# A hybrid encoder layer on one core: the input projections' stage reordered, and the scatter's row numbers computed beside the expert's output

## What is computed

```python
mod = silu(c) @ ada_w + ada_b                  # six rows of 1024: sh1, sc1, gt1, sh2, sc2, gt2
u = layer_norm(x) * (1 + sc1) + sh1
p_rw, p_conv, p_gate = split(u @ w_in)         # 27 + 16 + 16 tiles of 128 columns
p_rw = p_rw + mu_prev*(prev - p_rw) + mu_next*(next - p_rw)      # neighbours in time
h = h_a * sigmoid(h_b)                         # h_a, h_b: halves of p_conv
h = silu(layer_norm(depthwise_conv31(h)))
y_b = h @ cpw_w + cpw_b
y_a = rwkv7(p_rw)                              # scans in both directions
x1 = layer_norm(alpha*x + (1 + gt1) * ((g_a*y_a + g_b*y_b) @ w_o))
u2 = layer_norm(x1) * (1 + sc2) + sh2
# each token goes to 8 of 64 experts, F = 256, and to one shared expert:
y = sum_k weight_k * (silu(u2 @ gate_e) * (u2 @ up_e)) @ down_e + shared
out = layer_norm(alpha*x1 + (1 + gt2) * y)
```

## Time and profile before

| | us |
|---|---|
| median of three runs | 2157.51 |
| lowest, highest | 2155.03, 2160.31 |
| the profiled execution | 2165.9 |
| its span, first to last instruction | 2164.2 |
| TensorE busy | 1928.5 (89% of the span) |
| VectorE busy | 1399.5 (65%) |
| ScalarE busy | 880.3 (41%) |
| GpSimd busy | 660.9 (31%) |
| mean granted clock of TensorE | 0.956 of 2.4 GHz |

### The profile page before, as it was taken

How to read it: one execution, slowest core, us unless ns; L and a number is a source line. 1 busy time by engine, 2 the same in 40 slices (tenths; PEclk the granted TensorE clock), 3 DMA queues, 4 the chain that set the end, 5 groups by cost and what they waited for, 6 DMA issues and landing times. The chain is left out here.

```text
span 2164.2 us, 54389 instructions
## 1 busy us (share of the span) xinstructions
PE 1928.5 (89%) x20438; PEld 1424.8 (66%) x20438; DVE 1399.5 (65%) x2791; ACT 880.3 (41%) x1464; POOL 660.9 (31%) x533
## 2 busy tenths in 40 slices
PE   5699999978399999999997788999999999999966
PEld 1576777746298998999894355666666666666632
DVE  2688788844254656565642847777777777777717
ACT  0322232222245454555431005555555555555501
POOL 4545444301534344434410301221122222122213
PEclk9899999989599999999998888999999999999988
DMA  5644554214200010001005118899889888888845
GB/s 198 209 132 145 179 167 151 80 53 132 70 21 10 17 32 26 26 14 32 14 14 189 65 51 342 325 344 328 329 323 337 314 318 328 315 326 326 319 168 215
DMA packets 161938, 377.90 MB, mean 175 GB/s; under 512 B 23572, under 2 KB 97474, under 8 KB 134385
## 3 DMA queue, kind: packets, MB, share of 16 engines
q1 hardware_dynamic: 140292, 337.50, 43.6%
q0 software_dynamic: 21152, 37.80, 4.9%
q10 hardware_dynamic: 335, 0.22, 0.0%
HBM read 361.00 MB, written 53.24 MB: 191 GB/s over the span
## 5 line engine op out<-in xcount | busy, mean ns | idle before, releaser
L1991 DVE TENSOR_TENSOR moe_w_lo<-moe_raw,moe_w_hi 128x1024 fp32r<-128x1024 f32 x272 | 315.0, 1221 | 2.5 <-ACT moe_w_hi L1910 2.1
L1910 ACT ACTIVATE moe_w_hi<-moe_raw 128x1024 fp32r<-128x1024 f32 x272 | 265.3, 1047 | 85.8 <-DMA moe_raw<-in_exp_up 83.9
L1854 PE MATMUL moe_pH<-moe_w_hi,moe_x_hi 128*128 128x512 f32 x544 | 221.1, 406 | 38.7 <-DVE moe_x_lo L1998 29.4
L1788 POOL DMA_INDIRECT moe_xg<-scratch_u2d,moe_idx x70 | 70.9, 1012 | 588.5 <-issue 513.4
L1864 PE MATMUL moe_pY<-moe_wd,moe_hT 128*128 128x512 f32 x544 | 244.8, 593 | 0.5 <-ACT moe_hT L1925 0.5
L419 POOL TENSOR_TENSOR proj_w_lo<-proj_w,proj_w_hi 128x1024 fp32r<-128x1024 f32 x59 | 177.2, 3008 | 211.3 <-ACT proj_w_hi L503 211.3
L621 DVE SCALAR_TENSOR_TENSOR proj_hc<-proj_hp,cwT,proj_hc 128x256 f32 x480 | 232.3, 557 | 7.9 <-DVE proj_st L594 7.9
L446 PE MATMUL proj_bank<-proj_u_hi,proj_w_hi 128*128 128x512 f32 x536 | 211.9, 395 | 24.5 <-DVE proj_u_lo L652 12.2
L1854 PE MATMUL moe_pH<-moe_w_hi,moe_x_lo 128*128 128x512 f32 x544 | 213.8, 393 | 0.0
L1854 PE MATMUL moe_pH<-moe_w_lo,moe_x_hi 128*128 128x512 f32 x544 | 213.5, 393 | 0.0
L446 PE MATMUL proj_bank<-proj_u_hi,proj_w_lo 128*128 128x512 f32 x536 | 210.6, 393 | 0.0
(11 more groups left out here) (337 smaller groups left out, 3679.5 us busy)
## 6 DMA issues: line engine op xcount, KB each, us to landing
moe_raw<-in_exp_gate SPq DMA_DIRECT2D x69, 1024.0 KB, 7.0
moe_raw<-in_exp_up SPq DMA_DIRECT2D x69, 1024.0 KB, 10.0
moe_wd<-in_exp_down SPq DMA_DIRECT2D x68, 1024.0 KB
proj_w<-in_w_in SPq DMA_DIRECT2D x59, 512.0 KB, 4.6
proj_aw<-in_ada_w SPq DMA_DIRECT2D x8, 2048.0 KB, 8.2
last_yb<-scratch_ybuf SPq DMA_DIRECT2D x4, 2560.0 KB, 25.0
mod_aw<-in_ada_w SPq DMA_DIRECT2D x4, 2048.0 KB, 19.6
scratch_rkv<-proj_st SPq DMA_DIRECT2D x24, 256.0 KB, 2.2
```

The lines of the kernel that those rows point to most:

```text
L1788: pool.indirect_dma_start(out=xg[q][:], out_offset=None, in_=g["u2d"][:], in_offset=bass.IndirectOffsetOnAxis(ap=idx[q][:, 0:1], axis=0), ...
L1854: ins = nc.tensor.matmul(pH[:], a[:, k], w[p][:, k].rearrange("p w f -> p (w f)"), start=(k == 0 and n == 0), stop=(k == KC - 1 and n == 2))
L1910: nc.scalar.activation(w_hi[p][:, ks].rearrange("p k w f -> p w k f"), raw[p][:, :, ks], ACT.Copy) \
L1991: nc.vector.tensor_tensor(w_lo[p][:, ks].rearrange("p k w f -> p w k f"), raw[p][:, :, ks], w_hi[p][:, ks].rearrange("p k w f -> p w k f") ...
```

## The change

Three stages' code is touched.

In `modulation_and_norm` the modulation is made as columns: ada_w is the stationary operand in pieces of 128x128 and one column of silu(c) the moving one, 4 x 8 matmuls for each of the four loaded groups of 512 columns, in two halves (groups 0 and 2, then 1 and 3). Each half's bias is added from a transposed row, and four of the eight channel tiles of u are turned and scaled after each half; the way over memory is gone. The stage also makes the high and low halves of u, loads the first five tiles of w_in, makes four high and two low halves of them, and xn takes x's place.

In `projections_and_conv` the loop over trips is replaced by one list of 67 tiles in another order (hb and ha alternating, then ga, gb, then r, k, v, then lora, then cpw), with four slots for halves, five for raw weights, six PSUM banks and six slots for stores. VectorE makes all low halves instead of GpSimd. The taps are 512 wide, two channel tiles alternate, and a planner (`tap_plan`) gives each tile's place a quota of them. The convolution's mean is made in four parts between products, centring to silu beside later products. The other modulation rows are made like the first ones: eight pieces of 4 x 8 matmuls with 128x128 stationary and one moving column, after tiles 20, 23, ... 41. gb stays in SBUF in u1T's place.

In `moe` place_y is gone: the destination rows are written in read_y, directly before the output's second half, `gcol` and the semaphore y_ready are gone, and ScalarE and VectorE take the weight from `val`.

```diff
 def modulation_and_norm(...)
+        bcol = s.sb("bcol", [P, 2, KC])
+        u1 = g["u1T"]
...
-            for n in range(NG):
+            for n in (0, 2, 1, 3):
                 sp.dma_start(aw[:, n], ada_w[0, :, n * GROUP:(n + 1) * GROUP]...).then_inc(aw_in[n], 16)
-            sp.dma_start(bias[:], ada_b[:, 0:2 * D]).then_inc(b_in, 16)
-            sp.wait_ge(row_done, NG)
-            sp.dma_start(g["mod"][:, 0:2 * D], row[:]).then_inc(row_out, 16)
-            sp.wait_ge(row_out, 16)
-            for n in range(2):
-                sp.dma_start(mod[:, n], columns(g["mod"][0, n * D:(n + 1) * D])).then_inc(mod_in, 16)
+            for n in range(RAW):
+                sp.dma_start(g["w"][:, n], weight_tile(w_in, None, n)).then_inc(w_pre, 16)
...
+            for k in range(KC):                                          # ScalarE
+                act.wait_ge(tp_used, k + 1)
+                nc.scalar.activation(g["u_hi"][:, k], u1[:, k], ACT.Copy).then_inc(tp_high, 1)
+            act.wait_ge(w_pre, 16 * RAW)
+            for n in range(SPLIT):
+                nc.scalar.activation(g["w_hi"][:, n], g["w"][:, n], ACT.Copy).then_inc(w_high, 1)
...
-            for n in range(NG):                                          # TensorE
-                pe.wait_ge(aw_in[n], 16)
-                for k in range(KC):
-                    ins = nc.tensor.matmul(acc[n][0:1, :], g["csil"][:, k:k + 1], aw[:, n, k], ...)
+            for h in range(2):
+                for n in (h, 2 + h):
+                    pe.wait_ge(aw_in[n], 16)
+                    for m in range(GROUP // P):
+                        col = (n // 2) * 4 + m
+                        for k in range(KC):
+                            ins = nc.tensor.matmul(acc[h][:, col:col + 1], aw[:, n, k, m * P:(m + 1) * P], g["csil"][:, k:k + 1], ...)
                 ins.then_inc(mod_done, 1)
+                if h == 0:
+                    pe.wait_ge(xn_done, TT)
+                for k in range(4 * h, 4 * h + 4):
+                    ...
+                    turn(k)
...
+TILES = [(kind, i) for i in range(KC) for kind in ("hb", "ha")] \
+    + [("ga", i) for i in range(KC)] + [("gb", i) for i in range(KC)] \
+    + [(kind, i) for i in range(KC) for kind in RKV] + [("lora", j) for j in range(3)]
+N_U = len(TILES)
+TILES += [("cpw", n) for n in range(KC)]
+RAW, SPLIT, BANKS_P, N_ST = 5, 4, 6, 6
+MOD_AFTER = list(range(20, 44, 3))
+def tap_plan():
+    work = {"ha": 0.7, "r": 1.7, "k": 1.7, "v": 1.7, "lora": 1.7}
+    quota, ends, credit, done = [], [], 0.0, 0
+    for n in range(N_U):
+        credit += 5.45 + (3.6 if n in MOD_AFTER else 0.0) - 1.3 - (work.get(TILES[n - 1][0], 0.0) if n else 2.5)
+        there = 2 * CW * (n // 4)
+        q = max(0, min(int(credit / 0.67), there - done, KC * CW - done))
...
 def projections_and_conv(...)
-            def modulate(i):
-                for k in range(KC):
-                    ins = nc.tensor.matmul(pstat[0:1, :], g["csil"][:, k:k + 1], aw[:, k], ...)
+            def modulate(c):
+                pe.wait_ge(aw_at[c % 2], 16 * (c // 2 + 1))
+                for m in range(MC):
+                    col = c * MC + m
+                    for k in range(KC):
+                        ins = nc.tensor.matmul(pmod[:, col:col + 1], aw[:, c % 2, k, m * P:(m + 1) * P], g["csil"][:, k:k + 1], ...)
+                ins.then_inc(S["mod_done"], 1)
+            for n in range(N):
+                product(n)
+                for q in range(KC // 2):
+                    if n == ends[q] + 1:
+                        mean(q)
+                if n in MOD_AFTER:
+                    modulate(MOD_AFTER.index(n))
...
+                if n == E_CONV + 3:
+                    variance()
...
+            def high_h():                                                # ScalarE, before the cpw tiles
+                act.wait_ge(S["tile_done"], N_U)
+                for k in range(KC):
+                    act.wait_ge(S["silu"], k + 1)
+                    nc.scalar.activation(u_hi[:, k], hc[:, k], ACT.Copy).then_inc(S["h_high"], 1)
...
+            for n in range(N + 1):                                       # VectorE
+                if n == N_U:
+                    split_h()
+                if n >= 1:
+                    evict(n - 1)
+                if SPLIT <= n + 3 < N:
+                    low(n + 3)
+                if n < N_U:
+                    taps(quota[n])
...
 def moe(...)
             def read_y(b, q, n):                                         # ScalarE
                 act.wait_ge(d_done, 2 * b + 1)
-                act.wait_ge(y_ready, b + 1)
+                act.wait_ge(i_ready, b + 1)
                 act.wait_ge(y_free[q], n + 1)
-                nc.scalar.activation(y[q][:, 0:512], pY[0][:], ACT.Copy, scale=gcol[q][:, 0:1]).then_inc(y0_read, 1)
+                nc.scalar.activation(y[q][:, 0:512], pY[0][:], ACT.Copy, scale=val[:, bass.ds(b, 1), 2]).then_inc(y0_read, 1)
-            def place_y(b, q, n):                                        # VectorE
-                v.wait_ge(y_free[q], n + 1)
-                v.wait_ge(y0_read, b)
-                ch.mark(nc.vector.tensor_scalar(sidx[q][:], val[:, bass.ds(b, 1), 1], float(NO_ROW), None, ALU.add))
-                nc.vector.tensor_copy(gcol[q][:], val[:, bass.ds(b, 1), 2]).then_inc(y_ready, 1)
             def read_y(b, q, n):
                 v.wait_ge(y_free[q], n + 1)
                 v.wait_ge(d_done, 2 * b + 2)
-                v.wait_ge(y_ready, b + 1)
-                nc.vector.tensor_scalar(y[q][:, 512:D], pY[1][:], gcol[q][:, 0:1], None, ALU.mult).then_inc(y1_read, 1)
+                ch.mark(nc.vector.tensor_scalar(sidx[q][:], val[:, bass.ds(b, 1), 1], float(NO_ROW), None, ALU.add))
+                nc.vector.tensor_scalar(y[q][:, 512:D], pY[1][:], val[:, bass.ds(b, 1), 2], None, ALU.mult).then_inc(y1_read, 1)
             def body(b, p, i):
                 ...
                 read_y(b - 1, 1 - p, i + (p - 1))
-                place_y(b, p, i)
```

More of the change, by code:

```diff
@@ new lines, in projections_and_conv @@
+        st = s.sb("st", [P, N_ST, T])
+        gb = g["u1T"]
+        rs = s.sb("rs", [P, T])
+        bank = [s.ps(f"bank{i}") for i in range(BANKS_P)]
+        pstat, pmod = s.ps("pstat"), s.ps("pmod")
+        w_at = [s.sem(f"w_at{i}") for i in range(RAW)]
+        aw_at = [s.sem(f"aw_at{i}") for i in range(2)]
+        stored = [s.sem(f"stored{i}") for i in range(N_ST)]
+        taken = [s.sem(f"taken{i}") for i in range(BANKS_P)]
+        names = """w_high w_low tile_done base_done padded taps conv_done mean_done cent sq_done var_done std_done
+            rs_done nrm silu h_high h_split mod_done modc_done turned mrow_done mod_out brow_in""".split()
@@ new lines, in _ @@
+            sp.dma_start(brow[:], ada_b[0, 2 * D:].rearrange("(r p) -> r p", p=P)).then_inc(S["brow_in"], 16)
+            for n in range(RAW, N + RAW + 3):
+                if n < N:
+                    load(n)
+                if n == RAW + 2:
+                    load_mod(0)
+                if n == RAW + 4:
+                    load_mod(1)
+                m = n - RAW - 3
+                if m in slot_of:
+                    store(m)
+                if m in MOD_AFTER and MOD_AFTER.index(m) + 2 < KC:
+                    load_mod(MOD_AFTER.index(m) + 2)
+                if m == N_U:
+                    sp.wait_ge(S["mrow_done"], 1)
+                    sp.dma_start(g["mod"][0, 2 * D:].rearrange("(r p) -> r p", p=P), mrow[:]).then_inc(S["mod_out"], 16)
@@ L441, in _ @@
+            for slot in range(N_ST):
+                sp.wait_ge(stored[slot], 16 * len([n for n in keeps if slot_of[n][0] == slot]))
+            sp.wait_ge(S["mod_out"], 16)
         @block.tensor
         def _(pe):
-            def product(o, j, k):
-                for n, (a, b) in enumerate(((w_hi, u_hi), (w_lo, u_hi), (w_hi, u_lo))):
-                    ins = nc.tensor.matmul(o[:], a[:, j, k], b[:, k], start=(k == 0 and n == 0),
-                                           stop=(k == KC - 1 and n == 2))
-                return ins
@@ L467, in _ @@
-            for j in range(NK):
-                project(j, 0, None)
-            modulate(0)
-            with pe.Fori(1, KC) as i:
-                for j in range(NK):
-                    project(j, i, i)
-                modulate(i)
-            for j in range(3):
-                project(j, KC, KC)
-            pe.wait_ge(mod_read, KC + 1)
-            pe.wait_ge(h_used, KC + 1)
-            for k in range(KC):
-                ins = nc.tensor.matmul(pstat[:], g["mean1024"][:], hc[:, k], start=(k == 0), stop=(k == KC - 1))
@@ new lines, in high_h @@
+            def high_h():
+                act.wait_ge(S["tile_done"], N_U)
+                for k in range(KC):
+                    act.wait_ge(S["silu"], k + 1)
+                    nc.scalar.activation(u_hi[:, k], hc[:, k], ACT.Copy).then_inc(S["h_high"], 1)
+            for n in range(N):
+                if n == N_U:
```

(18 more changed lines are left out.)

552 lines of the change are left out of this document (236 added, 316 removed).

## The result

The changed kernel takes 2188.2 us (median of five runs, 2176.16 to 2194.12) against 2160.31 us of the kernel before (five runs beside it, 2155.03 to 2163.97): ratio 1.0118, 95% interval 1.0095 to 1.0141. It is slower by 28 us, where 2150 was forecast. The profiled execution is the fastest of the five (2176.16), so a sum over its stages comes out 12 us low.

The account below looks back on a forecast made before the run. TensorE, 89% busy, was taken as the bound. Terms +18.3, +26.7, -1 and -51.6 sum to -7.6: profiled 2165.9 becomes 2158.3, less 8.4 to the median gives 2150 us; range 2080 to 2202, the forecast's own 2118 to 2187.

Parts of the forecast that it names:

- The opening: Opening: the modulation's weight loads run at half clock, first product at 91.8 instead of 73.47: +18.3 us.
- The modulations in the projections: Projections: eight modulations between products lose the full clock, 13.5 us each, 108 in all; stage +26.7 us.
- The convolution's norm under the products: Projections: centring, squares, root and silu run beside products; 1.7 us lost before the first cpw tile.
- Rival (d): Projections: VectorE becomes the bound if a tap costs over 0.8 us; up to 2200 us; chance 0.04 together with others.
- The experts: Experts' stage: without VectorE's wait landings get quicker and the block period falls from 11.2 to 10.45 us: -51.6 us.
- Rival (a): Experts: GpSimd's serial gather, scatter, landing keeps the period at 11.2 us, decisive if above 10.55; 2201 us; chance 0.19.
- (b): Opening and projections: TensorE's clock does not fall, opening -8, projections -20; 2077 us; chance 0.12.
- (c): Opening and projections: clock kept and a modulation costs only the planner's 3.6 us; 2036 us; chance 0.03.

Follow-up runs that it names:

- the front alone: The changed kernel with the old experts' stage, so only opening and projections are changed; median 2202.93 us, ratio 1.0184 to the kernel before.
- the late landing and the added wait: The changed kernel, GpSimd waiting for scatter b-2's landing, its sign ahead of the scatter, gather held until hidden(b+1) is done; 2146.47 us, ratio 0.9922.
- The small doses: The changed kernel with the projections' 256 modulation pairs in 32 pieces of 8, one after each of tiles 20 to 51; 2152.55 us, ratio 0.9938.
- the late landing alone: The changed kernel with GpSimd waiting for the landing of scatter b-2 instead of b-1; median 2171.93 us, ratio 1.0053 to the kernel before.

## Why the prediction was wrong

**The opening** was right, with its reason: half clock, 0.213 us a load, first product at 90.87 for a forecast of 91.8. The terms that the prediction names add to 91.1, not 91.8 (84.6 + 1.4 + 4.2 + 0.9), so 0.7 us of the forecast has no term behind it.

**The modulations in the projections** were right in mechanism and a little dear: 10.5 and 2.2 behind make 12.7 where 13.5 was forecast, 6 us in all. The full clock lasted 3 us into the first, as taken (2.9). The scan came at +34.9 against +44; by medians, with the front alone, the whole kernel lost 40.

**The convolution's norm under the products** was right. No tile waits for a low half, and the one wait ahead of the cpw tiles is 1.5 us. Rival (d) did not come.

**The experts** are the step that failed: "I take 10.45 as the period, nearer the unhindered row: -51.6". The period came out at 10.86 in the changed kernel's profile, its fastest run; by medians the edit gave -22 alone and -15 in the changed kernel. The mechanism I had named is shown in part: in the good stretch landings are quicker (7.4 instead of 8.3) and most blocks take 10.25. That the place among the loads is the reason is not shown there, since the gather starts 2.8 us after the issue of gate and up in the good stretch and 2.4 in the kernel before; only the run with the late landing and the added wait moves the place on purpose. What failed was to take the good stretch as where the chain comes to rest. Nothing holds it there. Gather and scatter (2.6 us) and a landing of 4.3 to 12.0 come to the period or over it, so a few slow landings push GpSimd past the good place, landings there are 9.3, the lag grows until a gather is late, and TensorE loses 3 us and part of its clock (granted 0.72 on average over the 6.2 us behind). With the landing taken out of the series this lag and the wide spread are gone. The wait that I saw removed had been the regulator: with it the mean stayed at 11.2. Rival (a), the serial chain, had the right cause at 0.19, and the period stayed above its mark of 10.55, but its price was too high; the result lies between it (2201) and the forecast. I had both numbers, the sum of 11 us and the spread 4.9 to 11.8, and read the spread as a chance for gain alone.

The forecast's own range fails with it: its bounds for the experts, -65 to -22, leave out the -15, and with those for the front they add to 2120.5 to 2195.5, not to the 2118 to 2187 that it states.

**Rivals (b) and (c)**, clock kept, fell with the first stretch at 0.50. The small doses show that they were wrong about the run of pairs, not about the pair.

The Trainium skill (TensorE: Matmul & The Clock Gate, Part 1) says that the clock follows how busy TensorE has been. By the reading under which every instruction counts, the modulation should have kept it; the stretch from 212.50, with TensorE busy 7.90 of 7.90 us and the clock at 0.50, speaks against that reading. What it counts instead no run here shows.

## What to carry to other kernels

A matmul with one moving column was no cheaper here than its weight load (0.107 us a pair at full clock), and a run of 64 of them cost TensorE its full clock, for itself and for what followed. Use the form with many moving columns, or strew the pairs between wide products in doses as small as here (1.8 us); both took 44 us off the stage.

A wait on the path may be what keeps a serial helper in step. Before removing it, add up the helper's own chain with its slowest transfers, not the median; if that exceeds the period, take the landing out of the chain first. Then try where among the large loads the small transfers start: together this gave a median 30 us under the changed kernel's fastest run (2146.5 against 2176.2), and a spread of 3 us.

## What the runs showed of the hardware that was not expected

A DMA share of 0.93 with 342 GB/s (the kernel with the late landing alone, 1520 to 1620 us) looked like a limit while blocks were 10.7 apart; the same work ran at 0.97 and 372 GB/s when gather and scatter started 5.6 us later, with TensorE never idle (1420 to 1520 us).

The granted clock that the profile prints ahead of its first record is not a measured one. In the opening of the changed kernel,

```profile
24.78:52.00 27.22, 27.22 (x128) 27.22 (x129) 3.44 (x5) 0.21 (x1) 6.27 (x9) 1.00 0.67 226
52.08:55.40 3.32, 3.32 (x17) 3.32 (x18) 2.30 (x5) 1.12 (x2) 0.00 (x0) 1.00 0.00 0
55.45:79.55 24.10, 24.10 (x130) 24.10 (x129) 2.20 (x4) 1.35 (x3) 0.00 (x0) 0.57 0.00 1
```

the first two stretches print 1.00, yet loads go 0.213 apart as at 0.50, and the 16 transposes take 3.53 where the earlier trace rows have 1.97. Only the third has a record: 3.4 us at full clock from 55.3 on (loads 0.112 apart), then half. Where the printed clock and the distance of loads differ, I go by the distance.
